# A streaming encoder step with gathered experts: keys and values of past tiles in DRAM, attention on visible blocks, ten gather buffers

## The reference, cut to what matters

```python
h = rmsnorm(x, g_attn_norm)
z = h @ w_in                                  # q rank 384, kv rank 256, rope 32, 3 x 512 conv
q = rmsnorm(c_q, g_q) @ w_uq                  # 8 heads x (64 + 32), rope on the 32
kv = concat(past_kv, rmsnorm(c_kv, g_kv)) @ w_ukv   # keys 8 x 64, values 8 x 64
mask = k_chunk[None, :] <= (q_pos // 64)[:, None]   # a query sees its own chunk of 64 and earlier ones
p = softmax(where(mask, q @ k.T * 96 ** -0.5, -1e30))
attn = p @ v
x = x + concat(rmsnorm(attn), rmsnorm(b_gate * conv3(c_gate * u_conv))) @ w_out
# experts: per token 8 heads, each the 16 best of 128 x 128 product keys
s_top, i_top = top_k(q_peer @ peer_keys, 16)  # twice per head, then the best 16 of the 256 sums
a = gelu(peer_u[experts] . h2)                # 128 experts a token, rows of 1024
x = x + sum(softmax(best) * a * peer_v[experts])
y = rmsnorm(x, g_final)
```

## Time and profile before

| | |
|---|---|
| median of 3 runs | 3784.34 us |
| profiled execution, its own time | 3783.47 us |
| its span, first to last instruction | 3781.7 us |
| TensorE, VectorE, ScalarE, GpSimd busy | 71%, 60%, 39%, 31% |
| moved by DMA | 1293.78 MB, 342 GB/s over the span |
| mean granted TensorE clock | 0.842 |

### The profile page before, as it was taken

The page is one execution under the profiler, slowest core; times in us unless marked ns, Lnnn a source line. Parts: engine busy times, 40 slices in busy tenths (PEclk is TensorE's granted clock), DMA queues, the critical chain, the costliest instruction groups (busy, mean ns, idle before and its releaser), DMA issues.

```text
span 3781.7 us, 41104 instructions
## 1 busy us (share of the span) xinstructions
PE 2674.7 (71%) x12828; PEld 1422.3 (38%) x12828; DVE 2268.3 (60%) x5882; ACT 1456.1 (39%) x3849; POOL 1171.7 (31%) x1071
## 2 busy tenths in 40 slices
PE   7668766677668776677667876678666876587867
PEld 5335333343325333343234433254233433263431
DVE  2674567545684557645684557745675456735674
ACT  2233533344333533335333443335333453335333
POOL 1133332333232332324223342323323342313223
PEclk9789988888778988789888997898878898777669
DMA  5689999999899998899898998999989998968888
GB/s 206 260 341 364 379 341 355 364 353 358 318 354 364 361 379 326 342 361 374 334 358 354 365 384 329 352 351 366 348 349 363 353 375 328 355 250 326 304 298 345
DMA packets 208375, 1293.78 MB, mean 342 GB/s; under 512 B 26944, under 2 KB 28512, under 8 KB 72992
## 3 DMA queue, kind: packets, MB, share of 16 engines
q0 software_dynamic: 152064, 1107.36, 75.8%
q1 hardware_dynamic: 56096, 183.81, 13.0%
HBM read 1276.58 MB, written 5.55 MB: 339 GB/s over the span
## 4 chain that ended last, share of the span: by engine, by line
DMA 29%; PE 29%; DVE 25%; issue 9%; ACT 6%; POOL 2%; SPq 0%; DVEq 0%; POOLq 0%; ACTq 0%
DMA ring<-in_peer_uv,idx_peer 16%; PE acc L819 13%; DMA wst<-in_w_blocks 8%; DVE ring L1298 8%; PE Sps L574 5%; DMA hf_half<-hf_front 3%; POOL ring L524 2%; PE M L558 2%; ACT diag L856 2%; DVE bufA L1265 1%; DVE bufA L1074 1%; DVE eab L1267 1%; DVE bufA L1263 1%; DMA ring<-in_peer_uv,idx_pack 1%; PE Sps L714 1%
## 5 line engine op out<-in xcount | busy, mean ns | idle before, releaser
L1298 DVE CUSTOM_DVE_ANT_0 ring<-ring,hf_half 128x1024 f32<-128x1024 f32 x1024 | 1245.6, 1221 | 861.4 <-DMA ring<-in_peer_uv,idx_peer 788.0
L819 PE MATMUL acc<-ring,diag 128*64 128x512 f32 x4096 | 1251.1, 742 | 703.9 <-ACT diag L856 702.6
L524 POOL DMA_INDIRECT ring<-in_peer_uv,idx_peer x896 | 992.3, 1107 | 2023.5 <-PE acc L819 1646.6
L819 PEld LDWEIGHTS acc<-ring,diag 128*64 128x64 f32 x4096 | 295.7, 161 | 1261.2 <-ACT diag L856 830.7
L982 ACT ACTIVATE dots<-dots 128x2 f32<-128x2 f32 x512 | 103.8, 203 | 1298.0 <-DVE dots L1298 1277.1
L775 PEld LDWEIGHTS M<-actT,wst 128*128 128x128 f32 x2304 | 299.1, 210 | 72.0 <-issue 65.1
L775 PE MATMUL M<-actT,wst 128*128 128x128 f32 (+1 forms) x2304 | 315.9, 294 | 5.7 <-DMA wst<-in_w_blocks 4.3
L574 PE MATMUL Sps<-actT,wst 128*128 128x128 f32 (+1 forms) x1728 | 254.4, 308 | 91.5 <-DMA wst<-in_w_blocks 90.5
L856 ACT ACTIVATE diag<-fold,dots 128x64 f32<-128x64 f32 (+1 forms) x1056 | 310.7, 340 | 19.8 <-PE acc L830 2.2
L524 POOL DMA_INDIRECT ring<-in_peer_uv,idx_lead x128 | 132.9, 1039 | 512.2 <-PE acc L819 231.5
L574 PEld LDWEIGHTS Sps<-actT,wst 128*128 128x128 f32 x1728 | 236.9, 219 | 139.8 <-DMA wst<-in_w_blocks 111.3
(11 more groups left out here) (187 smaller groups left out, 2625.9 us busy)
## 6 DMA issues: line engine op xcount, KB each, us to landing
wst<-in_w_blocks SPq DMA_DIRECT2D x297, 512.0 KB
ring<-in_peer_uv,idx_peer POOLq DMA_INDIRECT x896
hf_half<-hf_front SPq DMA_DIRECT2D x32, 256.0 KB
x_front<-in_x_p SPq DMA_DIRECT2D x8, 512.0 KB
w_out_sb<-in_w_out SPq DMA_DIRECT2D x8, 512.0 KB, 5.7
o_y_p<-qT SPq DMA_DIRECT2D x8, 512.0 KB
ring<-in_peer_uv,idx_lead POOLq DMA_INDIRECT x128
w_uq_sb<-in_w_uq SPq DMA_DIRECT2D x3, 384.0 KB, 4.6
```

The costliest lines, as they stand in the source:

```text
L524: pool.indirect_dma_start(ring[g % RING][:, :], None, a["peer_uv"], bass.IndirectOffsetOnAxis(ap=src[:, c:c + 1], axis=0)).then_inc(s_g[g ...
L819: mm = pe.matmul(acc[j * HALF_T:(j + 1) * HALF_T, half * 512:(half + 1) * 512], diag[:, at:at + HALF_T], ring[(SLOTS * t + 2 * m + j) % RI ...
L1298: dve.tensor_tensor_reduce(u, u, hf[:, :], 1.0, 0.0, ALU.mult, ALU.add, dots[:, k:k + 1]).then_inc(s_dot, 1)
```

## The change

- `kT`, `vv` and the 1024-wide `mask` are gone. `k_new` and `v_new` hold the keys and values of the tile at hand only. At step 24 SP stores them to DRAM (`store_kv`; for the sample, the two past blocks are stored at steps 9 and 14).
- In the attention of tile t, SP loads the keys of head h for the tiles before (`k_dram`, 96 partitions x 128t columns) into one of the weight buffers, and the values of two heads together into one of two `v_old` buffers. `USES` lists weights and key loads in one order.
- Scores, maximum, Exp, turns and value products run over the t + 1 visible blocks. Only the own block is masked, by a matmul of the identity with a mask tile onto the scores. The maximum is a plain reduce out of PSUM, and Exp reads PSUM.
- `WBUF` 2 to 3, a load placed when the use three before it is due, at most 12 steps ahead. `RING` 6 to 10. `FS` 94 to 104 (so `OWN` 24), `SAMPLE_SPAN` 85 to 95. Steps of the sample's past blocks and of its own key stage move by 1 to 4.
- The scratch for GpSimd's descriptors goes from 2048 to 4096.

```diff
-WBUF = 2
-RING = 6
+WBUF = 3
+RING = 10
-FS = 94
+FS = 104
-SAMPLE_SPAN = 85
-PAST_STEPS = {6: ((0, 0),), 8: ((0, 1), (0, 2)), 9: ((1, 0),), 11: ((1, 1),), 13: ((1, 2),)}
+SAMPLE_SPAN = 95
+PAST_STEPS = {6: ((0, 0),), 8: ((0, 1), (0, 2)), 11: ((1, 0),), 12: ((1, 1),), 13: ((1, 2),)}
+PAST_STORED = {9: 0, 14: 1}
+def earlier(t):
+    return PAST // P if sample(t) else t
+def uses():
+    listed = []
+    for t in range(TILES + 1):
+        own = [(BLOCK_STEP[b], t, "w", b) for b in STREAMED]
+        if t > 0:
+            own += [(ATT_STEP + 4 * h, t, "k", h) for h in range(H)]
+        listed += sorted(own)
+    return listed
+def load_step(i):
+    if i < WBUF or USES[i - WBUF][1] != USES[i][1]:
+        return 0
+    return max(USES[i - WBUF][0], USES[i][0] - 12)
...
 SP
+            def load_use(i):
+                step, t, kind, which = USES[i]
+                if i >= WBUF:
+                    before, tb, kb, wb = USES[i - WBUF]
+                    if kb == "w":
+                        sp.wait_ge(s_wused, BLOCKS * tb + wb + 1)
+                    else:
+                        sp.wait_ge(s_sc, H * tb + wb + 1)
+                if kind == "w":
+                    sp.dma_start(wst[i % WBUF][:, :], a["w_blocks"][which - (which > NARROW)]).then_inc(s_w[i % WBUF], 16)
+                else:
+                    if which == 0:
+                        sp.wait_ge(s_kvd, 32 * (TILES + 1 if sample(t) else t))
+                    n = earlier(t) * P
+                    sp.dma_start(wst[i % WBUF][0:QK, 0:n], (k_past if sample(t) else k_dram)[which][:, 0:n]
+                                 ).then_inc(s_w[i % WBUF], 16)
+            def load_v(t, q):
+                if q >= 2:
+                    sp.wait_ge(s_pv, H * t + 2 * (q - 2) + 2)
+                elif t > 1:
+                    sp.wait_ge(s_pv, H * (t - 1) + 2 * (q + 2) + 2)
+                if q == 0:
+                    sp.wait_ge(s_kvd, 32 * (TILES + 1 if sample(t) else t))
+                n = earlier(t) * P
+                sp.dma_start(v_old[q % 2][:, 0:n], (v_past if sample(t) else v_dram)[q][:, 0:n]).then_inc(s_v[q % 2], 16)
+            def store_kv(n, k_dst, v_dst):
+                sp.wait_ge(s_kv, 3 * n + 3)
+                sp.dma_start(k_dst.rearrange("h d k -> d h k"), k_new_v[0:QK, :, :]).then_inc(s_kvd, 16)
+                sp.dma_start(v_dst.rearrange("q p c -> p q c"), v_new_v).then_inc(s_kvd, 16)
+                if k == 24 and t < TILES - 1:
+                    store_kv(t, k_dram[:, :, t * P:(t + 1) * P], v_dram[:, :, t * P:(t + 1) * P])
+                for q in range(0 if first(t) else H // 2):
+                    if k == (25 + q if q < 2 else ATT_STEP + 8 * q - 7):
+                        load_v(t, q)
...
 TensorE
-                            pe.wait_ge(s_sm, H * t + h)
+                            pe.wait_ge(s_p, H * t + h)
+                        mm = pe.matmul(Sps[:, old:old + own], q_h, k_new_v[0:QK, h, 0:own], start=True, stop=sample(t))
+                        if not sample(t):
+                            mm = pe.matmul(Sps[:, old + CHUNK:old + P], ident[:, :], mask_tile[:, CHUNK:P],
+                                           start=False, stop=True)
+                        i = USE_AT[t, "k", h]
+                        pe.wait_ge(s_w[i % WBUF], 16 * (i // WBUF + 1))
+                        for lo in range(0, old, 512):
+                            n_keys = min(512, old - lo)
+                            mm = pe.matmul(Sps[:, lo:lo + n_keys], q_h, wst[i % WBUF][0:QK, lo:lo + n_keys],
+                                           start=True, stop=True)
+                        if h % 2 == 0:
+                            pe.wait_ge(s_v[h // 2 % 2], 16 * (2 * (t - 1) + h // 4 + 1))
...
 ScalarE
+                    if n > 0:
+                        act.wait_ge(s_pv, H * min(n, TILES))
+                        act.wait_ge(s_kvd, 32 * (n if n < TILES else n - 1))
-                        act.activation(bufA[:, 0:nk], bufA[:, 0:nk], ACT.Exp, bias=nm[:, h:h + 1], scale=SCALE,
+                        if h > 0:
+                            act.wait_ge(s_pTps, 2 * H * t + 2 * h)
+                        act.activation(bufA[:, 0:nk], Sps[:, 0:nk], ACT.Exp, bias=nm[:, h:h + 1], scale=SCALE,
...
 VectorE
-                        dve.tensor_tensor_reduce(bufA[:, 0:nk], Sps[:, 0:nk], mask[:, 0:nk], 1.0, LOWEST, ALU.add, ALU.max,
-                                                 mx[:, h:h + 1]).then_inc(s_sm, 1)
+                        dve.tensor_reduce(mx[:, h:h + 1], Sps[:, 0:nk], AX.X, ALU.max).then_inc(s_sm, 1)
```

More of the change, by code:

```diff
@@ L107, in front_steps @@
     return [(nxt, k - OWN)]
-def key_blocks(t):
-    return PAST // P + 1 if sample(t) else KB
+def earlier(t):
[8 more added lines that the diff above has]
+    return listed
+USES = uses()
+USE_AT = {use[1:]: i for i, use in enumerate(USES)}
+def load_step(i):
+    if i < WBUF or USES[i - WBUF][1] != USES[i][1]:
+        return 0
+    return max(USES[i - WBUF][0], USES[i][0] - 12)
 def sample(t):
@@ L166, in build @@
         cols = sb("cols_sb", NCOLS)
-        kT = sb("kT", H * KEYS)
-        vv = sb("vv", KB * H * VD)
+        k_new = sb("k_new", H * P)
+        v_new = sb("v_new", H * VD)
+        v_old = [sb(f"v_old{i}", (TILES - 1) * P) for i in range(2)]
+        k_dram = nc.dram_tensor("k_dram", (H, QK, SEQ - P), F32).ap()
+        v_dram = nc.dram_tensor("v_dram", (H // 2, P, SEQ - P), F32).ap()
+        k_past = nc.dram_tensor("k_past", (H, QK, PAST), F32).ap()
+        v_past = nc.dram_tensor("v_past", (H // 2, P, PAST), F32).ap()
         w_narrow = sb("w_narrow_sb", KC * ROPE)
@@ L197, in build @@
         csb = sb("csb", 2 * P)
[L198 to L200 removed]
+        mask_tile = sb("mask_tile", P)
         ident = sb("ident", P)
@@ L289, in build @@
         s_rc = sem("s_rc")
-        s_mask = sem("s_mask")
+        s_kvd = sem("s_kv_in_dram")
+        s_v = [sem(f"s_v_loaded{i}") for i in range(2)]
         s_sc = sem("s_scores")
@@ L405, in front @@
                     sp.dma_start(rope[:, :], a["rope"][bass.ds(t * P, P), :]).then_inc(s_rope, 16)
-                for b in STREAMED:
-                    if max(0, BLOCK_STEP[b] - 4) == k:
-                        load_block(t, b)
+                for i, use in enumerate(USES):
+                    if use[1] == t and load_step(i) == k:
+                        load_use(i)
+                if sample(t) and k in PAST_STORED:
+                    b = PAST_STORED[k]
+                    store_kv(TILES + b, k_past[:, :, b * P:(b + 1) * P], v_past[:, :, b * P:(b + 1) * P])
+                if k == 24 and t < TILES - 1:
[3 more added lines that the diff above has]
+                        load_v(t, q)
                 if sample(t) and k == 4:
@@ L699, in front @@
                             mm = pe.matmul(M1[:, h * VD:(h + 1) * VD], bufB[:, h * P:(h + 1) * P],
-                                           vv[:, h * VD:(h + 1) * VD], start=True, stop=True)
+                                           v_new[:, h * VD:(h + 1) * VD], start=True, stop=True)
                         mm.then_inc(s_pv, H)
-                nb = key_blocks(t)
+                nb = earlier(t) + 1
+                own = tokens(t)
+                old = (nb - 1) * P
                 for h in range(0 if first(t) else H):
                     k0 = ATT_STEP + 4 * h
+                    q_h = qT[0:QK, h * P:(h + 1) * P]
                     if k == k0:
@@ L708, in front @@
                             pe.wait_ge(s_conv, CC * t + CC)
+                            pe.wait_ge(s_kv, 3 * n + 3)
                         else:
[L711 to L715 removed]
+                            pe.wait_ge(s_p, H * t + h)
[9 more added lines that the diff above has]
+                                           start=True, stop=True)
                         mm.then_inc(s_sc, 1)
@@ L724, in front @@
                         for c in range(nb):
-                            mm = turn(Tb[c // 4][:, (c % 4) * P:(c % 4 + 1) * P], bufA[:, c * P:(c + 1) * P])
+                            wide = own if c == nb - 1 else P
+                            mm = turn(Tb[c // 4][0:wide, (c % 4) * P:(c % 4 + 1) * P], bufA[:, c * P:c * P + wide])
                             if c == nb - 1 or c == 3:
@@ L730, in front @@
                         pe.wait_ge(s_pTb, H * t + h + 1)
-                        for c in range(nb):
-                            mm = pe.matmul(M1[:, h * VD:(h + 1) * VD], bufB[:, c * P:(c + 1) * P],
-                                           vv[:, (c * H + h) * VD:(c * H + h + 1) * VD],
-                                           start=(c == 0), stop=(c == nb - 1))
-                        mm.then_inc(s_pv, 1)
+                        if h % 2 == 0:
+                            pe.wait_ge(s_v[h // 2 % 2], 16 * (2 * (t - 1) + h // 4 + 1))
+                        for c in range(nb - 1):
+                            pe.matmul(M1[:, h * VD:(h + 1) * VD], bufB[:, c * P:(c + 1) * P],
```

(12 more changed lines are left out.)

70 lines of the change are left out of this document (21 added, 49 removed).

## The result

The changed kernel takes 3592.95 us (median of 4 runs, 3589.19 to 3601.29) against 3782.24 us for the kernel before: ratio 0.9511, 95% interval 0.9478 to 0.9544. The forecast was 3635 us in a range of 3560 to 3750. The profiled execution has a span of 3587.4 us, 194.3 us less than before.

The account below looks back on a forecast made before the run. Transfers were taken to set the pace in slots 36 to 115, VectorE in the top-16 searches. 7 x (-15 - 6) + 22 - 22 - 7 + 5 = -149 gave a span of 3633 and 3635 us, range 3560 to 3750.

Parts of the forecast that it names:

- (a): Slots 36 to 115: more gather and weight buffers raise the DMA share; 241 us against 256, -15 us a body.
- more than forecast: Rival: transfers reach 397 GB/s and TensorE's relief lets them; -24 us a body, time 3572; chance 0.16.
- (b): Keys and values through DRAM: 3.2 MB a body in the transfer-bound stretch at 385 GB/s, 8 us, inside the -15.
- (c): Attention on visible blocks only: costed at nothing, hidden by transfers; could bring some 10 us a body.
- (d): New waits for key and value loads and stores: cost 0 in attention, +5 us for the kernel from the sample tile.
- The prediction's own sign of being wrong: Attention: TensorE showing waits for key loads of some us per head would mean the prediction is wrong.
- (e): Fronts 10 slots sooner: hf copies in 8 us for 13.86, -6 us a boundary; body 0 +22, last body -22.
- Slots 0 to 25 near 88 us: Expected sign: top-16 search stretches at the front of a body stay unchanged at 3.5 us per slot.
- (f): Start-up: the third weight buffer takes away most weight gaps between products, -7 us (bounds 0 and -15).
- Last body: Body with the sample's fronts: -22 us from sooner fronts, +5 us from the sample's store waits; near 485 us.
- crowding of SP's queue: Rival: SP's transfers slow with the gathers in flight, 10/6 times; +11 us a body, time 3860; chance 0.08.
- the rate would not rise: Rival: gaps in slots 36 to 115 come from memory or uneven engines; 363 GB/s, time 3719; chance 0.22.

Follow-up runs that it names:

- the late store: Changed kernel with the store of new keys and values moved from step 24 to step 62, behind the attention's loads in SP's queue: 3565.41 us, ratio 0.9426.

## Why the prediction was right, and where it was not

The time lies in the range, 42 us below the forecast, and the sign was right. So was the main cause, that transfers set the pace and that more gathers in flight quicken them. That the sum for bodies 0 to 6 is so near (-125 forecast, -135 measured) is in part luck, as three errors in it cancel. By the start times of the dot products the transfer-bound slots (36 to 115 before, 26 to 105 after) gave -137.5 us where -105 was forecast, the boundaries (slots 126 and 127) +30.4 instead of -42, and the search slots -27.3 instead of +22. Of the 45 us by which the spans differ from the forecast, 31 lie in the last body, 10 in bodies 0 to 6 and the rest in the start-up and the end. By its steps:

- *(a) ten buffers, three weight buffers.* Right. Slots 26 to 105 take 236.1 us in body 3 against 241 forecast, 256.0 before. The terms that were mis-sized are the rate and the gathers carried in advance. The four windows moved 3.3 + 31.4 + 40.5 + 18.9 = 94.0 MB in 236.1 us, 398 GB/s, 403 at a share of 1 where I took 385 (the rows' own mean share is 0.94, which gives 387). I had taken the rate at full share as a constant and expected only the share to rise. It rose with depth: the share hardly differs between six and ten buffers, the GB/s do. The bytes were 94.0 MB and not 92.0: of the 4.2 MB that four more buffers were to take out of the stretch some 2.3 went. The rival "more than forecast" had the rate right, 397 GB/s, and that transfers could use it though TensorE has its own work; I had held TensorE's 78 us in the input product against it, and at the higher clock they were 71. Over the whole span the mean 8 KB record of the gathers' queue is 338 ns before, 335 with six buffers in the changed kernel and 326 with ten, while the medians are 309, 309 and 313: with fewer gathers in flight it is some long records that make the mean. Why, no run here shows.
- *(b) 3.2 MB a body at full price.* It stands: with the late store the attention window grows from 92.3 us in body 0 to 106.8 in body 6 (start times of the dot products), 14.5 us for six steps of 0.655 MB, or 271 GB/s at the margin, dearer than the 385 GB/s that I used. The growing attention itself is not the likely cause: with the same growing blocks read from SBUF (visible blocks in the kernel before, six gather buffers) that window does not grow (100.8 us in body 0, 98.1 in body 6). That small rows and their turns make the loads dear is likely and not shown by itself.
- *(c) visible blocks at nothing.* Right for the kernel before: ratio 1.0021 alone.
- *(d) new waits at nothing.* Wrong. I reckoned the slack in steps and the landings at 7 to 13 us from the earlier trace rows, and did not count the turns: the store is small in bytes (0.655 MB) and large in rows (1280). It cost 28 us. The prediction's own sign of being wrong was a wait of some us per head; the profile has 90.5 us in 12 places, so 7.5 us where it occurs. For the sample tile ScalarE waits 12.5 us in two places for the past blocks' stores, inside the 0 to 26 that I had bounded; what of it reached the end was not measured.
- *(e) -6 us a boundary.* Wrong in sign, the step that failed outright: 20.8 became 25.1 us, and the hf copies land after 18.83 us where they landed after 13.86 before body 3, and after 17.82 instead of 12.85 at its end. I had forecast 8. I argued that a ring filled in time would leave the copies alone on the engines. But a ring of ten isn't full at the boundary: the stretch ahead of it, 1694.4 to 1761.9, is at a share of 1.01, and the window of the boundary itself at 1.02. The +22 for body 0 and the -22 for the last body were right to the microsecond by the experiment with the fronts at slot 34. As that trade is neutral and the boundary dearer, the sooner front is a loss of 19 us. "Slots 0 to 25 near 88 us" came out at 82.9, against 87.3 with six buffers and 83.1 with eight. So the search slots got shorter with depth too (3.49 us a slot with six buffers, 3.31 with ten, slots 2 to 25 of body 3), though VectorE waits for gathers there only 2 us even with six; how, stays open.
- *(f) start-up.* -9.1 against -7.
- *Last body.* -47.9 against -22 + 5, where most of the 42 us comes from. With the fronts at slot 34 it is -26 (508.3 to 482.2), from the other edits, which I had not given it, since its DMA share looked free at 0.82. Most of that is depth: with six gather buffers in the changed kernel this body is 35 us longer (488.1 against 453.2 from its first to its last dot product), with two weight buffers 10.

Of the rivals, crowding of SP's queue came true in part, in a form that I had not priced: weight loads of 4 KB rows land in 8.2 us with ten buffers, 8.3 with six, but stores of 512-byte rows land after 27.9 and 37.2 us with ten and 17.7 and 21.7 with six. I had argued that engines which alternate between queues would keep a longer queue of gathers from pushing SP's transfers back. They do alternate; but by the counts beside the stores (1479 and 2539 records with six buffers, 2001 and 1998 with ten) SP's rows pass in good part alone with six, and with ten each pays its turn. The hand-over of hf was lengthened by the sooner fronts and not by the depth. That the rate would not rise (with the Trainium skill, DMA: Bandwidth & Descriptors, Where 436 GB/s comes from, which puts the bound near 358 GB/s) is refuted by 420 GB/s in a 45 us window. What the Trainium skill's HBM Reference (Specifications (TRN2)) gives for a core alone, near 425 GB/s, agrees with that window.

## What to carry to other kernels

Where one queue streams large rows and fills the DMA engines, price another queue's transfers in rows, not bytes: here each of the small rows waited for one of the large ones, 0.28 us, as long as large ones were queued. Put what nobody waits for (here the store for the next tile) behind what somebody does, in the same queue. And when transfers set the pace, a wait removed elsewhere comes back in good part as a wait for transfers: 86 us of waits for keys were worth 28, and 65 us of waits for hf some 11, which is within the intervals.

## What the runs showed of the hardware that I had not expected

- The share of busy DMA engines is not a measure of the rate: at 0.97 body 3's attention ran at 369 GB/s with six gather buffers and at 383 with ten.
- The engines alternate between GpSimd's and SP's queues row by row, as far as counts show it (434 and 432 records in 8 us, at 3.16 and 0.22 MB; 14 and 15 in 0.31 us). The same 0.655 MB of stores land after 3.6 and 4.9 us with no gather moving and after 27.9 and 37.2 us beside ten gather buffers.
